# The filler products that TensorE runs at the joints of stages are left out of a two-block transformer kernel

## The reference, cut to what matters

```
def first_block(x, ...):                  # 2 layers
    h = rms_norm(x, g_mix); z = h @ w_in  # projections of three mixers and their gates
    o_a = mla_mixer(...)                  # latent attention, 8 heads
    o_b = conv_mixer(...)                 # gated, depthwise convolution of 31 taps, layer_norm
    o_c = nsa_mixer(...)                  # compressed, selected and window attention
    x = x + (g_a * o_a + g_b * o_b + g_c * o_c) @ w_out
    x = x + square(relu(rms_norm(x) @ w_ff1)) @ w_ff2
def second_block(x, c, positions, ...):   # 2 layers, then a last rms_norm
    mod = c @ mod_w + mod_b               # shifts, scales and gates from a condition vector
    h = rmsnorm(x) * (1 + sc1) + sh1
    x = x + g1 * mixer(h)                 # sparse top-k attention and forgetting attention, gated, @ w_out
    h = rmsnorm(x) * (1 + sc2) + sh2
    x = x + g2 * conv_ffn(h)              # up to 2 x 2816, convolution of 3 taps, silu gate, down
return rmsnorm(x)
```

## Time and profile before

| | |
|---|---|
| median of 3 runs | 3584.23 us (3581.09 to 3584.91) |
| the profiled execution's own time | 3583.43 us |
| its span, first to last instruction | 3581.7 us |
| TensorE (PE) busy | 3437.8 us, 96% |
| its weight loads (PEld) | 2818.8 us, 79% |
| VectorE (DVE), ScalarE (ACT), GpSimd (POOL) busy | 56%, 40%, 44% |
| mean granted TensorE clock | 0.981 of full |
| mean DMA rate | 97 GB/s |

### The profile page before, as it was taken

One profiled execution on the slowest core, in us unless ns is written; L12 is line 12 of the kernel. 1 busy time (PEld: TensorE's weight loads), 2 busy tenths in 40 slices (PEclk: granted clock), 3 DMA queues, 4 the chain that ended last, 5 costly groups with the idle time before them and its releaser, 6 DMA issues. The chain is left out here.

```text
span 3581.7 us, 44753 instructions
## 1 busy us (share of the span) xinstructions
PE 3437.8 (96%) x15838; PEld 2818.8 (79%) x15838; DVE 2015.3 (56%) x3260; ACT 1436.2 (40%) x2516; POOL 1586.3 (44%) x827
## 2 busy tenths in 40 slices
PE   7999999999999999999999999999999999999998
PEld 6877787788888777878887877778877877778877
DVE  5775655112367756641224666658964666658953
ACT  3256743232333567332323446233333446333332
POOL 3346453444444563534443641335543641335543
PEclk9999999999999999999999999999999999999999
DMA  4311123222232111322343221432343221432322
GB/s 165 103 57 37 36 89 106 93 94 95 88 124 97 45 42 46 114 83 94 106 146 108 72 89 60 165 112 103 131 153 107 72 89 56 164 112 104 134 89 94
DMA packets 96746, 346.62 MB, mean 97 GB/s; under 512 B 12624, under 2 KB 13264, under 8 KB 95952
## 3 DMA queue, kind: packets, MB, share of 16 engines
q1 hardware_dynamic: 96592, 344.62, 27.9%
HBM read 338.15 MB, written 6.29 MB: 96 GB/s over the span
## 5 line engine op out<-in xcount | busy, mean ns | idle before, releaser
L234 POOL TENSOR_TENSOR weights_lo<-arena,weights_hi 128x1024 fp32r<-128x1024 f32 x467 | 1189.8, 2548 | 1616.9 <-ACT weights_hi L208 1468.4
L208 ACT ACTIVATE weights_hi<-arena 128x1024 fp32r<-128x1024 f32 x491 | 517.8, 1055 | 622.7 <-PE ps L648 388.1
L302 PE MATMUL ps<-moving_hi,weights_hi 128*128 128x512 f32 x2256 | 568.8, 395 | 11.7 <-ACT weights_hi L208 6.7
L302 PE MATMUL ps<-moving_lo,weights_hi 128*128 128x512 f32 x2256 | 559.5, 390 | 0.0
L302 PE MATMUL ps<-moving_hi,weights_lo 128*128 128x512 f32 x2256 | 557.7, 389 | 0.0
L302 PEld LDWEIGHTS ps<-moving_hi,weights_hi 128*128 128x128 f32 x2256 | 424.1, 189 | 103.3 <-ACT weights_hi L208 7.1
L302 PEld LDWEIGHTS ps<-moving_lo,weights_hi 128*128 128x128 f32 x2256 | 424.1, 189 | 88.3
L302 PEld LDWEIGHTS ps<-moving_hi,weights_lo 128*128 128x128 f32 x2256 | 423.3, 188 | 87.2
L255 DVE TENSOR_TENSOR moving_lo<-arena,moving_hi 128x512 fp32r<-128x512 f32 x196 | 178.0, 959 | 230.9 <-ACT moving_hi L250 230.9
L2331 DVE SCALAR_TENSOR_TENSOR arena<-ps,arena 128x512 f32 x64 | 44.1, 691 | 306.7 <-PE ps L302 292.6
L1015 ACT ACTIVATE arena<-ps,arena 128x512 f32<-128x512 f32 (+1 forms) x320 | 165.9, 525 | 114.8 <-DVE arena L979 114.6
(11 more groups left out here) (384 smaller groups left out, 5259.6 us busy)
## 6 DMA issues: line engine op xcount, KB each, us to landing
arena<-wstream SPq DMA_DIRECT2D x532, 512.0 KB, 3.3
arena<-modw SPq DMA_DIRECT2D x64, 512.0 KB, 3.7
arena<-modw_first SPq DMA_DIRECT2D x32, 512.0 KB, 4.1
layer_input<-arena SPq DMA_DIRECT2D x2, 2048.0 KB, 6.9
arena<-layer_input SPq DMA_DIRECT2D x2, 2048.0 KB, 8.0
arena<-xT SPq DMA_DIRECT2D x4, 512.0 KB, 5.5
outT<-arena SPq DMA_DIRECT2D x8, 256.0 KB, 2.1
arena<-con SPq DMA_DIRECT2D x1, 1413.5 KB, 9.4
```

The costliest lines, as they stand in the source:

```text
L208: m.nc.scalar.activation(m.w_hi[:, j % 2, :], slab(m, base + at), ACT.Copy).then_inc(hi_ready, 1)
L234: m.nc.gpsimd.tensor_tensor(m.w_lo[:, j % 2, :], slab(m, base + (j if at is None else at)), m.w_hi[:, j % 2, :].bitcast(F32), ALU.subtract)\
L302: mm = m.nc.tensor.matmul(bank, unit_tile(w, k), a[:, k, :], start=(p == 0 and k == 0), stop=(p == 2 and k == KD - 1))
```

## The change

`keep_busy` and its 17 calls are removed. Every wait stays where it is. In the merge stage the branch is turned round, because its other arm is empty.

```diff
-def keep_busy(m, bank, count):
-
-    for _ in range(count):
-        m.nc.tensor.matmul(m.ps[:, bank, 0:2 * P], m.con("ident", P), m.con("ident", 2 * P), start=True, stop=True)
-
@@ linear_stage
                 pe.wait_ge(dve_evac, len(mine["dve"]) + 1)
-                keep_busy(m, 0, 3)
@@ down_stage
                 for p, (w, a, ready) in enumerate((hi_hi, lo_hi, hi_lo) if first and half == 0 else (hi_hi, hi_lo, lo_hi)):
-                    if half == 0 and first and p == 0:
-                        keep_busy(m, 7, 2)
...
                 pe.wait_ge(updated, 1)
-                keep_busy(m, 0, 8)
@@ norm_stage
             mm.then_inc(summed, 1)
-            if squared_before:
-                keep_busy(m, 2, 3)
...
             mm.then_inc(spread_done, 1)
-            if squared_before:
-                keep_busy(m, 2, 1)
@@ attention_stage
-            keep_busy(m, 0, 2)
@@ merge_stage
             pe.wait_ge(gated, 8 * (NB - 1) + 2)
-            if not modulate:
-                keep_busy(m, 0, 3)
-            else:
+            if modulate:
@@ head_norm_stage
-            keep_busy(m, 6, 2)
@@ first_front_stage
             pe.sem_inc(chunk_done, 1)
-            keep_busy(m, 4, 2)
...
             pe.wait_ge(k_out, 4)
-            keep_busy(m, 5, 2)
@@ compressed_attention_stage
             fill.begin(pe)
-            keep_busy(m, 6, 1)
...
-            keep_busy(m, 0, 1)
@@ gate_stage
             pe.wait_ge(evaced, count - BANKS + 1)
-            keep_busy(m, count % BANKS, 2)
@@ squared_up_stage
-            keep_busy(m, 6, 3)
@@ second block: front
             pe.sem_inc(chunk_done, 1)
-            keep_busy(m, 3, 2)
@@ second block: up
             pe.sem_inc(chunk_done, 1)
-            keep_busy(m, 6, 2)
...
             over_partitions(m, [acc_mod], 5).then_inc(mod_summed, 1)
-            keep_busy(m, 6, 4)
```

## The result

The changed kernel takes 3596.98 us (median of 8 runs, 3590.41 to 3601.54); the kernel before, run beside it, 3583.29 us (8 runs, 3581.02 to 3586.81). The ratio is 1.0038, with a 95% interval of 1.0027 to 1.0049: +13.7 us, slower. The profiled execution has a span of 3594.9 us, 13.2 more than before.

What follows compares the result with a forecast made beforehand. TensorE was taken as the bound, with its clock falling to half rate behind empty pauses. Losses of 21.8 us less gains of 4.6 gave net +17.2 us on 3583.43, forecast as 3600 us, range 3589 to 3611.

Steps and rivals of the forecast that it cites:

- (a): Up to down, four joints: the dense stage behind each pause pays the full 1.7 us fall, 6.8 us lost.
- (b): Norm to first products, five joints: half-rate start loses 3.5 us at three, 0 at two before the second block's up stage.
- (c): Into the first block's attention and compressed attention, four joints: falls of 1.4 and 1.1 us, 5.0 us lost.
- (d): Attention to gates and gates to merge, eight joints: half of them fall at 1.1 us, 4.4 us lost.
- (e): Merge to out and out to up, four joints: three fall at 0.69 us, 2.1 us lost.
- gains: Norm stages and ends of the gates: removing fillers that are late themselves saves 4.6 us.
- The 4.93 us wait: Second block's up stage, amid first products: TensorE's wait for a high part of weights hides their lateness, 0 us lost.
- The fillers' own time: Rival, norm stages and gate ends: fillers overrunning the release decide, so removal gives 3579 us; chance 4 in 100.
- Paid in full: Rival, 26 joints: every clock fall costs 1.7 us, 44 us less 4.6, giving 3623 us; chance 9 in 100.
- given back: Rival: the clock falls but most is hidden, 7.6 us lost, 3.0 net, 3586 to 3588 us; chance 11 in 100.

Runs made afterwards that it cites:

- e4_thin: The kernel before with every filler product cut from 256 columns to one, at the same places: 3591.07 us, ratio 1.0028.
- e3_rest: The changed kernel with fillers put back at all joints except those of up and down and those around the norm: 3585.33 us, ratio 1.0007.
- e8_again: The changed kernel run once more, unaltered, for a second profile: 3596.80 us, ratio 1.0039.
- e1_down: The changed kernel with fillers put back at the ends of both up stages and the beginning of down alone: 3589.55 us, ratio 1.0024.
- e2_norm: The changed kernel with fillers put back around the norm alone, including the beginnings of the stages behind it: 3592.28 us, ratio 1.0034.
- e6_trim: The kernel before with fillers cut in the norm and at the end of the gates, one added at the beginning of both fronts: 3573.81 us, ratio 0.9968.
- e9_hole: The kernel before with ten and not four fillers at the end of the second block's up stage: 3581.88 us, ratio 0.9994.
- e11_trim_again: The kernel before with overrunning fillers trimmed and one added at both fronts, the same trimmed kernel run once more: 3574.41 us, ratio 0.9976.

## Why the prediction was right, point by point

*Direction, size, mechanism.* 3600 us was forecast, 3597 measured; the net of +17.2 came out as +13.7. The mean clock came to 0.967, where about 0.965 was forecast. At the up-to-down joint TensorE's pause kept its length within 0.1 us, the clock fell behind it, and instructions at the same places with hardly any work in them (e4_thin) don't prevent it. That the sum came so near is in part luck. In the first profile its terms are 10.1 for (a), 3.4 for (b), 5.7 for (c), 0.6 for (d), -3.2 for (e) and 3.5 of gains, 13.1 us net against 13.2 of span: what (a) had too little, (d) and (e) had too much.

*(a) Up to down, 6.8 us.* Undersized. In the profile the four cost 2.73, 2.65, 2.35 and 2.38 us: half rate went on beyond the fall that I priced at 1.7. In the second profile they cost 1.56, 1.49, 2.36 and 2.37 us, 7.8 together. If the kernel before loses at the second block's two in other executions than the profiled one, which isn't shown, the change costs less there on average.

*(b) Norm to first products, 3.5 us and 0 at the second block's up stage.* Fronts +0.95, +1.31 and -0.20, 2.1 us in all; up stages +0.64 and +0.67. The 4.93 us wait hid the late first products wholly, as forecast: it shrank to 3.78 us and ended at the same distance from the stage's beginning. The 0.64 us come from behind it, where 16 products took 4.67 and not 4.03 us; that term I didn't have.

*(c) Attention and compressed attention, 5.0 us.* 5.7 us in the first profile, nearly 0 in the second. I took it that each of the four joints falls once by the change. At attention, behind the empty pause of 2.0 us, it fell at 2 of 8 joints (none of 14 with plain fillers); at compressed attention the clock had fallen with fillers too, at both joints of the profile of before, so that only a longer fall costs more. e3_rest shows that the group that holds them, with several other kinds of joint, is worth some 11 us.

*(d) Attention to gates to merge, 4.4 us.* Oversized in the profiles: one gate stage of four grew, by 0.55 us, and no merge did. That is the step of the sum that was wrong. I took half of the eight to fall; in the four profiles without fillers there it was 3 of 16 into the gates (a pause of 2.16 us) and none of 16 into the merge (1.7 us), though the pause of 2.09 us into the second block's attention, where it was empty, was followed by the fall at 21 of 22 joints.

*(e) Out and up, 2.1 us.* The falls came, their price did not. Into the first block's up stage the clock fell at all 8 joints without fillers at the end of out, and at 2 of 14 with plain ones. Yet that stage took 186.65 us in e8_again with 10.2 us at half rate, and 186.61 us before with 3.4: half rate at its beginning is hidden wholly, and not down to the 0.69 us that I took. Out is unchanged to 0.03 us in the first profile; behind its pause of 3.3 us the clock fell at 10 of 14 joints with fillers as well. The other up stage was 3.08 us shorter; that was chance, as it was near 185.0 us in e1_down, e2_norm and e6_trim as well, and long in the profile of before.

*Gains, 4.6 us.* The five norms gave -0.35, 0.93, 0.68, 1.39 and 0.93, 3.6 us against 3.5. The last norm, where I had a gain of 0.3, lost 0.75: its sums and diagonal products ran at half rate. That is not clearly the change's doing, since with all these fillers in place it took as long in e9_hole. The gates gave 0.2 to 0.3 each at three of four.

*The rivals.* The fillers' own time is real, and cutting the fillers that overrun, with one more at each front, is worth 9 us (e6_trim, e11_trim_again), twice what I worked out, of which the profiles place 5; as an account of the whole change it fell, since with every filler gone the clock takes that back and more. "Paid in full" fell with (d) and (e), "given back" with the measured ratio.

## What to carry to other kernels

Work that nobody reads can pay, if the engine is the bound behind the pause: look at the granted clock of the first microseconds after a wait, and compare twin stages. Fill a pause wholly and end before its release: with a hole of 3 us in the middle the clock fell at eight joints of ten, and fillers past the release cost up to 1.6 us in a norm stage. Where the clock's falls differ from one execution to the next, one profile is no account of a change; take stage lengths from several, and the whole from medians.

## What the runs showed of the hardware

The clock's fall behind a given pause is not fixed: the same kernel's attention stage took 57.51 us in one execution and 54.29 in another, compressed attention 38.34 and 37.01, with identical code and pauses. Nor does a pause's length settle it: 2.16 us empty were followed by half rate at 3 of 16 joints, 2.09 us at another place at 21 of 22, and 3.26 us once not at all. Behind a long pause half rate can go on into a second stretch (0.50 over 3.55 us, 0.69 over the next 3.35), and the stage then loses 2.4 to 2.7 us and not 1.7. Fillers of one column don't hold the clock, and float32 transposes of an identity mostly do (0.968 and 0.978 granted over the span, against 0.981 for products of 256 columns).
